# The soft-plus chain and the inner norm roots on GpSimd, an earlier weight split, and another order in the opening

## What is computed

```python
for l in range(DEPTH):                       # first block, DEPTH = 2
    n = rms_norm(h, norm1_w[l])
    proj = einsum('bld,de->ble', n, w_in[l])
    z, xbc, dt_f, dt_b, sc_b, sc_c, sc_v = split(proj)
    y_ssd = ssd_branch(z, xbc, dt_f, dt_b, ...)   # short conv, dt = softplus(dt + bias),
                                                  # a = -exp(a_log) * dt, decays, norm per group
    y_sc = short_conv_branch(sc_b, sc_c, sc_v, ...)
    h = h + einsum('ble,ed->bld', concat(y_ssd, y_sc), w_out[l])
    n = rms_norm(h, norm2_w[l])
    h = h + conv_ffn(n, ...)
...
for l in range(DEPTH):                       # second block
    # conv branch (31 taps, layer_norm), differential attention (rms_norm of each head),
    # block attention, gates, layer_norm, feed-forward with squared relu, layer_norm
```

## Time and profile before

| | |
|---|---|
| median of 3 runs (lowest to highest) | 1765.27 us (1764.46 to 1765.59) |
| the profiled execution's own time | 1764.93 us |
| its span, first to last instruction | 1762.9 us |
| TensorE busy | 1709.6 us (97%), x12334 |
| DVE busy | 1340.2 us (76%) |
| ACT busy | 921.5 us (52%) |
| GpSimd busy | 30.8 us (2%) |
| DMA, mean | 171 GB/s |

### The profile page before, as it was taken

How to read it: one execution, slowest core, us unless ns; L and a number is a source line. 1 busy time by engine, 2 the same in 40 slices (tenths; PEclk the granted TensorE clock), 3 DMA queues, 4 the chain that set the end, 5 groups by cost and what they waited for, 6 DMA issues and landing times.

```text
span 1762.9 us, 30277 instructions
## 1 busy us (share of the span) xinstructions
PE 1709.6 (97%) x12334; PEld 1580.0 (90%) x12342; DVE 1340.2 (76%) x2227; ACT 921.5 (52%) x1481; POOL 30.8 (2%) x51
## 2 busy tenths in 40 slices
PE   7999999999999999999999999999999999999997
PEld 6999889998999979999898998899989989989996
DVE  5867777777877867777798878866678988886666
ACT  5566555555656646555544654444344466453442
POOL 0000000000000000000000001000000000100000
PEclk9999999999999999999999999999999999999999
DMA  6544445555545445555465444555546635455552
GB/s 209 165 144 144 167 146 189 191 185 162 168 145 156 140 164 188 194 186 192 150 215 186 134 154 162 184 191 191 188 147 201 204 122 172 130 197 185 190 191 96
DMA packets 234055, 300.92 MB, mean 171 GB/s; under 512 B 6179, under 2 KB 199357, under 8 KB 233917
## 3 DMA queue, kind: packets, MB, share of 16 engines
q1 hardware_dynamic: 233609, 298.87, 52.0%
q10 hardware_dynamic: 308, 0.12, 0.0%
HBM read 293.72 MB, written 1.05 MB: 167 GB/s over the span
## 4 chain that ended last, share of the span: by engine, by line
PE 76%; DVE 17%; ACT 4%; issue 2%; DMA 0%; ACTq 0%; POOL 0%; DVEq 0%; POOLq 0%
PE bank L489 16%; PE bank L491 16%; PE bank L490 16%; DVE weights_lo L1420 7%; PE bank L567 5%; PE bank L568 5%; PE bank L569 5%; PE bank L539 2%; PE bank L540 2%; PE bank L541 2%; DVE conv_sums L1842 2%; ACT weights_hi L1017 1%; PE bank L689 1%; ACT pair L1280 1%; PE bank L594 1%
## 5 line engine op out<-in xcount | busy, mean ns | idle before, releaser
L489 PE MATMUL bank<-input_hi,weights_hi 128*128 128x256 f32 x2768 | 790.9, 286 | 12.8 <-DVE weights_lo L1420 6.5
L490 PE MATMUL bank<-input_lo,weights_hi 128*128 128x256 f32 x2768 | 783.7, 283 | 0.0
L491 PE MATMUL bank<-input_hi,weights_lo 128*128 128x256 f32 x2768 | 783.5, 283 | 0.0
L1420 DVE TENSOR_TENSOR weights_lo<-raw_weights,weights_hi 128x1024 fp32r<-128x1024 f32 (+1 forms) x554 | 649.8, 1214 | 138.3 <-ACT weights_hi L1017 136.1
L1017 ACT ACTIVATE weights_hi<-raw_weights 128x1024 fp32r<-128x1024 f32 (+1 forms) x554 | 546.3, 1036 | 331.8 <-PE bank L491 175.0
L489 PEld LDWEIGHTS bank<-input_hi,weights_hi 128*128 128x128 f32 x2768 | 531.1, 192 | 21.5 <-issue 17.7
L490 PEld LDWEIGHTS bank<-input_lo,weights_hi 128*128 128x128 f32 x2768 | 531.5, 192 | 1.8
L491 PEld LDWEIGHTS bank<-input_hi,weights_lo 128*128 128x128 f32 x2768 | 531.3, 192 | 0.0
L567 PE MATMUL bank<-weights_hi,hidden_hi 128*128 128x512 f32 x432 | 168.9, 391 | 0.2
L568 PE MATMUL bank<-weights_lo,hidden_hi 128*128 128x512 f32 x432 | 168.7, 390 | 0.0
L569 PE MATMUL bank<-weights_hi,hidden_lo 128*128 128x512 f32 x432 | 168.1, 389 | 0.0
(11 more groups left out here) (256 smaller groups left out, 1795.9 us busy)
## 6 DMA issues: line engine op xcount, KB each, us to landing
raw_weights<-in_w_in SPq DMA_DIRECT2D x105, 1024.0 KB, 5.3
raw_weights<-in_w_ff SPq DMA_DIRECT2D x64, 1024.0 KB, 5.3
raw_weights<-in_w_ffn_up SPq DMA_DIRECT2D x44, 1024.0 KB, 5.1
raw_weights<-in_w_ffn_down SPq DMA_DIRECT2D x22, 1024.0 KB, 5.0
raw_weights<-in_w_out SPq DMA_DIRECT2D x16, 1024.0 KB, 5.1
raw_weights<-in_w_o SPq DMA_DIRECT2D x8, 1024.0 KB, 5.1
pair<-pair SPq DMA_DIRECT2D x64, 64.0 KB, 2.9
raw_weights<-in_w_diff_out SPq DMA_DIRECT2D x4, 1024.0 KB, 5.1
```

The source lines that it names most:

```text
L489: mm(o, w_hi, x_hi, start=first, stop=False, skip_group_check=quiet)
L490: mm(o, w_hi, x_lo, start=False, stop=False, skip_group_check=quiet)
L491: return mm(o, w_lo, x_hi, start=False, stop=last, skip_group_check=quiet)
L1420: tt(wlo[:, t, r], raw[:, s, r], whi[:, t, r].bitcast(f32), SUB).then_inc(w_ready, 1)
```

## The change

The soft-plus steps move from DVE to a function `soft_plus` on GpSimd, ten instructions, with a power of -1 in place of the reciprocal. The thirteen small instructions of an inner norm become one on DVE, a wait, and a power of -0.5 on GpSimd (`spread_roots`). `split_hi(3)` and `split_lo(3)` move from the dt chunk to chunk 0: on ACT behind the middle tap and ahead of the tanh, on DVE behind the outer taps. In the opening TensorE multiplies zeros 20 times, turns the norm's output with ten multiplications of zeros in place of two, and turns the parameter rows after that. On GpSimd the token norms' roots and the clearing of `prow2` take their places between the new functions. Context lines are cut.

```diff
@@ -233,7 +233,8 @@
         small = sb("small", [P, 64])
-        minus_half = small[:, 63:64]
+        minus_half, minus_one = small[:, 56:64], small[0:32, 55:56]
+        spread_var, spread_root = ctx.enter_context(nc.semaphore("spread_var")), ctx.enter_context(nc.semaphore("spread_root"))
         one_hot = sb("one_hot", [P, 32], f32r)
@@ -593,7 +594,7 @@
-            def turned(r):
+            def turned(r, fillers=2):
@@ -603,7 +604,7 @@
                         turn(0, k)
-                keep_clock(2, ring[3])
+                keep_clock(fillers, ring[3])
                 for b in range(4):
@@ -611,18 +612,18 @@
             pe.wait_ge(zero_ready, 2)
-            keep_clock(16, ring[3])
+            keep_clock(20, ring[3])
             pe.wait_ge(ident_loaded, 16)
-            pe.wait_ge(rows_loaded, 16 * N_ROW_DMAS)
-            for l in range(DEPTH):
-                last = nc.tensor.transpose(ring[0][:, l * P:(l + 1) * P], prow[:, 3 * l, :], ident)
-            last.then_inc(pt_ready, 1)
-            keep_clock(4, ring[3])
...
                 cx, ux = l * C1, l * U1
-                turned(l * 2)
+                turned(l * 2, 10 if l == 0 else 2)
+                if l == 0:
+                    pe.wait_ge(rows_loaded, 16 * N_ROW_DMAS)
+                    for i in range(DEPTH):
+                        last = nc.tensor.transpose(ring[0][:, i * P:(i + 1) * P], prow[:, 3 * i, :], ident)
+                    last.then_inc(pt_ready, 1)
                 gemm_paced(0, cx, 0, ux, ring[0], l * 16)
@@ -945,14 +946,43 @@
             pool.memset(minus_half, -0.5).then_inc(half_ready, 1)
+            pool.memset(minus_one, -1.0).then_inc(half_ready, 1)
             pool.memset(in_cols[:], 0.0).then_inc(zero_ready, 1)
...
                     pool.wait_ge(var_ready, r * 2 + t + 1)
-                    nc.gpsimd.tensor_tensor(norm_small[:, 3, t:t + 1], norm_small[:, 2, t:t + 1], minus_half, ALU.pow).then_inc(root_ready, 1)
-            pool.wait_ge(half_ready, 1)
+                    nc.gpsimd.tensor_tensor(norm_small[:, 3, t:t + 1], norm_small[:, 2, t:t + 1], minus_half[:, 0:1], ALU.pow).then_inc(root_ready, 1)
+            def spread_roots(k, n):
+                pool.wait_ge(spread_var, k + 1)
+                nc.gpsimd.tensor_tensor(small[:, 24:24 + n], small[:, 16:16 + n], minus_half[:, 0:n], ALU.pow).then_inc(spread_root, 1)
+            def soft_plus(l):
+                x, u, w, ln, one, den, a = [dts[:, i, :] for i in range(5)] + [dta[:, i, :] for i in range(2)]
+                pool.wait_ge(dt_dve, l * 2 + 2)
+                chain(nc.gpsimd.tensor_scalar(one, w, 1.0, None, ALU.is_equal))
+                chain(nc.gpsimd.tensor_scalar(den, w, -1.0, None, ALU.add))
+                chain(nc.gpsimd.tensor_scalar(x, x, 0.0, None, ALU.max))
+                chain.sync()
+                chain(nc.gpsimd.tensor_tensor(den, den, one, ALU.add))
+                chain.sync()
+                chain(nc.gpsimd.tensor_tensor(den, den, minus_one.to_broadcast([32, SEQ]), ALU.pow))
+                pool.wait_ge(dt_act, l * 2 + 2)
+                chain(nc.gpsimd.tensor_tensor(one, one, ln, ALU.add))
+                chain.sync()
+                chain(nc.gpsimd.tensor_tensor(den, den, u, ALU.mult))
+                chain.sync()
+                chain(nc.gpsimd.tensor_tensor(den, den, one, ALU.mult))
+                chain.sync()
+                chain(nc.gpsimd.tensor_tensor(den, den, x, ALU.add))
+                chain.sync()
+                nc.gpsimd.tensor_scalar(a, den, pc1[0:32, P1["a_exp"]:P1["a_exp"] + 1], -1.0, ALU.mult, ALU.mult).then_inc(dta_ready, 1)
+            chain = Chain(pool, pool_chain)
+            pool.wait_ge(half_ready, 2)
             roots(0)
@@ -963,12 +993,17 @@
-            chain = Chain(pool, pool_chain)
             pool.wait_ge(skip_ready, 2)
-            for r in range(1, 2 * DEPTH - 1):
-                roots(r)
-            pool.wait_ge(y_done, HEADS // 2 * DEPTH)
-            pool.memset(prow2[:], 0.0).then_inc(rows2_zero, 1)
+            for k in range(4 * DEPTH):
+                if k and k % 4 == 0:
+                    roots(k // 2 - 1)
+                    roots(k // 2)
+                if k == 4 * DEPTH - 1:
+                    pool.wait_ge(y_done, HEADS // 2 * DEPTH)
+                    pool.memset(prow2[:], 0.0).then_inc(rows2_zero, 1)
+                if k % 4 == 0:
+                    soft_plus(k // 4)
+                spread_roots(k, TOK)
             pool.memset(hpad[:, :, 0:TAPS - 1], 0.0).then_inc(zero_ready, 1)
@@ -989,6 +1024,8 @@
             for l in range(DEPTH):
+                spread_roots(4 * DEPTH + 2 * l, 8)
+                spread_roots(4 * DEPTH + 2 * l + 1, TOK)
                 for m in range(4):
@@ -1145,7 +1182,6 @@
                         A(dts[:, 1, :], dts[:, 1, :], ACT.Exp).then_inc(dt_act, 1)
-                        split_hi(c + 2, cx, cr)
                         act.wait_ge(dt_dve, l * 2 + 2)
@@ -1156,8 +1192,8 @@
                     last.then_inc(conv_mid, 1)
-                    if 0 < c < 8:
-                        split_hi(c + 2, cx, cr)
+                    if c < 8:
+                        split_hi(c + 2 if c else 3, cx, cr)
                     act.wait_ge(ring_free, ux + (q + RING + 1))
@@ -1432,23 +1468,11 @@
-            def rsqrt_diagonals(sums, n, scale, signal):
-                v, y, t = small[:, 16:16 + n], small[:, 24:24 + n], small[:, 32:32 + n]
-                chain(ts(v, sums, scale, EPS, MUL, ADD))
-                chain.sync()
-                chain(ts(y.bitcast(i32), v.bitcast(i32), 1, None, ALU.arith_shift_right))
-                chain.sync()
-                chain(ts(y.bitcast(i32), y.bitcast(i32), -1.0, MAGIC, MUL, ADD))
-                chain(ts(v, v, -0.5, None, MUL))
-                chain.sync()
-                for _ in range(3):
-                    chain(tt(t, y, y, MUL))
-                    chain.sync()
-                    chain(tt(t, t, v, MUL))
-                    chain.sync()
-                    chain(stt(out=y, in0=t, scalar=1.5, in1=y, op0=ADD, op1=MUL))
-                    chain.sync()
+            def rsqrt_diagonals(k, sums, n, scale, signal):
+                y = small[:, 24:24 + n]
+                ts(small[:, 16:16 + n], sums, scale, EPS, MUL, ADD).then_inc(spread_var, 1)
+                dve.wait_ge(spread_root, k + 1)
                 for i in range(n):
@@ -1577,33 +1601,7 @@
-                x, w, u_, ln = dts[:, 0, :], dts[:, 2, :], dts[:, 1, :], dts[:, 3, :]
-                def steps_of_dt():
-                    one, den = dts[:, 4, :], dta[:, 0, :]
-                    dve.wait_ge(dt_dve, l * 2 + 2)
-                    chain(ts(one, w, 1.0, None, ALU.is_equal))
-                    yield
-                    chain.sync()
-                    chain(stt(out=den, in0=w, scalar=-1.0, in1=one, op0=ADD, op1=ADD))
-                    yield
-                    chain.sync()
-                    chain(V.reciprocal(den, den))
-                    dve.wait_ge(dt_act, l * 2 + 2)
-                    chain(tt(one, one, ln, ADD))
-                    yield
-                    chain.sync()
-                    chain(tt(den, den, one, MUL))
-                    yield
-                    chain.sync()
-                    chain(tt(den, den, u_, MUL))
-                    yield
-                    chain.sync()
-                    chain(stt(out=den, in0=x, scalar=0.0, in1=den, op0=ALU.max, op1=ADD))
-                    yield
-                    chain.sync()
-                    ts(dta[:, 1, :], den, pc1[0:32, P1["a_exp"]:P1["a_exp"] + 1], -1.0, MUL, MUL).then_inc(dta_ready, 1)
+                x, w, u_ = dts[:, 0, :], dts[:, 2, :], dts[:, 1, :]
@@ -1631,7 +1629,7 @@
                     dve.wait_ge(gstat, l * 4 + g + 1)
-                    rsqrt_diagonals(acc[2 + g % 2][:, 0:TOK], TOK, 1.0 / 256, gdiag)
+                    rsqrt_diagonals(l * 4 + g, acc[2 + g % 2][:, 0:TOK], TOK, 1.0 / 256, gdiag)
@@ -1679,17 +1677,14 @@
-                dt_steps = steps_of_dt()
                 for c in range(9):
...
                         stt(out=u_, in0=x, scalar=-1.0, in1=x, op0=MUL, op1=ALU.min).then_inc(dt_dve, 1)
-                        split_lo(c + 2, cx, halves=(0,))
                         dve.wait_ge(dt_act, l * 2 + 1)
                         ts(w, u_, 1.0, None, ADD).then_inc(dt_dve, 1)
-                        split_lo(c + 2, cx, halves=(1,))
                         continue
@@ -1697,14 +1692,8 @@
                                lambda tap, m: p1("xbc_w", 16 * tap + 2 * q + m), ring_free)
-                    if c > DT_CHUNK:
-                        next(dt_steps, None)
-                        next(dt_steps, None)
-                    if 0 < c < 8:
-                        split_lo(c + 2, cx)
-                    if c > DT_CHUNK:
-                        next(dt_steps, None)
-                        next(dt_steps, None)
+                    if c < 8:
```

(5 more changed lines are left out.)

## The result

The changed kernel takes 1819.88 us (median of 4 runs, 1819.72 to 1822.89) against 1765.36 us before: a ratio of 1.0313, 95% interval 1.030 to 1.0326. It is 3.1% slower, where I forecast 1755.7 and gave rival 1, a dear power, 0.22. The profiled execution took 1820.04 us with a span of 1818.2, so 55.3 us were added to the span.

What follows compares the result with a forecast made beforehand. TensorE bounds the kernel, busy 1709.6 of 1762.9 us. Gains 2.45 + 2.7 + 2.65 + 2.7 = 10.5, less 0.6 contention and 0.3 clock, give 9.6 us: 1755.7 us, range 1752 to 1775 (forecast's own 1752.5 to 1759.5).

Steps and rivals of the forecast that it cites:

- rival 1: Soft-plus on GpSimd: power dear, result late, costing twice what exceeds 10.3 us; 1775 at a 20 us power; chance 0.22.
- The power: GpSimd's 32x256 power in soft-plus: about 5 us, between bounds of 1.1 and 90 us, hidden behind chunks 3 to 5.
- the 10.3 us of time in hand: Soft-plus on GpSimd: time left for the power before TensorE needs the result at the end of chunk 5.
- The rival's break-even of 15 us: Soft-plus power on GpSimd: from about 15 us on, the change turns to a loss.
- The opening: Kernel start: twenty multiplications of zeros end at 7.9 to 8.0, `input_lo` starts at 14.1 instead of 16.59; gain 2.45 us.
- The sign that I had named: Opening: the prediction is wrong if the fillers, the ten multiplications between the tokens, run at 0.43 us.
- The split and the soft-plus: Chunks 3 to 5: wait for chunk 3 goes, 1.0 us ahead of chunk 4; gain 2.7 us layer 1, 2.65 layer 0.
- the recurrence: Step-by-step timing of chunks 3 to 5: chunk 5 starts at 464.65 instead of 467.33, in layer 0 46.2 instead of 48.86.
- The norms: Inner norms' roots on GpSimd: TensorE's waits on the diagonals, 1.6 us at L705 and 1.1 at L798, go; gain 2.7 us.
- Contention: DVE's splits beside GpSimd's plain soft-plus work: between 0 and 3.6 us a layer lost, taken as 0.3 a layer.
- The worse reading of it: DVE's splits beside the power: the power would shut them out for its whole length, speaking for the second rival, chance 0.12.

Runs made afterwards that it cites:

- the probe: Kernel before with six extra GpSimd instructions (five powers, one product, of several sizes) where GpSimd idles in layer 0: 1765.01 us.
- the split alone: Kernel before with only the early split of chunk 3: 1764.71 us against 1765.22, ratio 0.9998.
- the roots alone: Kernel before with only the inner norms' roots moved to GpSimd: 1761.74 us, ratio 0.9980.
- the power out: Changed kernel with the 32x256 power turned into a product, leaving out the soft-plus reciprocal: 1755.4 us against 1765.09, ratio 0.9943.
- the reciprocal in the gap: Changed kernel, full version, with comparison, denominator and reciprocal on DVE where it waited for ACT, other six soft-plus instructions on GpSimd: 1755.02 us, ratio 0.9942.
- 96 columns: Changed kernel with the power over the first 96 of 256 columns, the other reciprocals left out: 1773.42 us against 1765.05, ratio 1.0044.
- the soft-plus back on DVE: Changed kernel with the soft-plus steps back in their old places on DVE, other parts kept: 1760.05 us, ratio 0.9972.
- the opening alone: Kernel before with only the new opening: 1763.92 us, ratio 0.9996.

## Why the prediction was wrong

**The power: the step that failed.** "I take about 5 us: above the plain price several times over, nearer to the low end." It took 41.16. The bounds, 1.1 and 90 us, held it; the choice between them did not. The only row had one column, and its excess of 0.35 us over a plain instruction could be set-up or price. The added columns show that 0.159 us of it is paid by each. I let the range end at 1775, as if a power over 20 us need not be covered, though nothing in the trace excluded it. In the sum's terms: the 10.3 us of time in hand were nearly right (9.9 measured, 41.16 - 31.31), and the power's term of 5 us, taken as hidden, was eight times too small.

**The mechanism of rival 1 was right.** It said twice what exceeds 10.3 us, on top of 1755.7. With 41.16 us that is 61.7, so 1817.4, against 1819.9 measured. Missing are the 3.6 us of half clock behind the two stalls, which I had not priced. The rival's break-even of 15 us was too late as well: at 15.66 us the loss is already 8 us, for contention takes 2.1 us a layer of the time in hand and the lower clock another 1.5.

**The opening.** Right in kind, half in size: 1.3 us of 2.45 at `input_lo`. I took the point where the multiplications of zeros pass from 0.43 to about 0.24 us each from one execution. It wanders: sixteen took 5.05 us in that one, and 5.50, 6.20 and 5.29 in three others with the same opening (the probe, the split alone, the roots alone), and twenty took 6.75 to 7.24 us in six. So they end near 9.0 and hold up the first tokens. `input_lo` started between 16.12 and 17.67 with the old opening and between 14.78 and 15.27 with the new one, so the 1.3 us of the two profiled executions are one draw of a gain of 0.9 to 2.9. The sign that I had named, multiplications at 0.43 us, did come, but among the first twenty and not among the ten between the tokens. Alone the opening cannot be told from no change.

**The split and the soft-plus.** Right, step by step: the wait for chunk 3 gone, 0.96 and 0.95 us ahead of chunk 4 where I had 1.0, none ahead of chunk 5. Chunk 5 ends at 50.51 in layer 0; with 5.9 us a chunk it started at 44.6, 4.3 us earlier than before, of which the opening is 1.3 and this part 2.9 (forecast 2.65). In layer 1 it is 2.9 as well (forecast 2.7). That the early split alone is worth next to nothing (0.4 us in layer 1), and that nearly all of the gain needs both, lay in the recurrence but was not said.

**The norms.** 2.7 forecast, 3.5 measured alone, with an interval of 1.9 to 5.1. The powers of 0.70 and 1.65 us were within the bounds. Most of it comes from the first block (1.2 us a layer, where the waits that I added up were 0.8), little from the second (0.25, where they were 0.5); why, stays open.

**Contention.** Both engines slow down: 3.38 against 2.35 us on DVE, 1.58 against 0.71 on GpSimd. The Trainium skill (SBUF — State Buffer, "Who interferes with whom") states that a DVE instruction with two SBUF inputs contends with a GpSimd one that reads SBUF; the trace agrees. The worse reading of it, that the power would shut the splits out, is wrong here: they took 2.35 us beside it.

**The rest of the sum, and some luck.** 1755.7 were forecast for a power that is hidden, 1755.4 measured with the power out and 1755.0 in full with DVE's reciprocal. The terms do not all fit that well: the opening gave about 1.1 us less than its term, the split and the norms about as much more together, and these misses cancel.

## What to carry to other kernels

A function that one instruction evaluates element by element has a price per column that a one-column row cannot show; measure it at the width it will have, in the idle time of its engine, before its result goes on TensorE's path. Where the bounds of such a price lie nearly two powers of ten apart, the time in hand decides, and the chance of missing it belongs near one half. And free a list before moving work up in it: the earlier split gained next to nothing until the soft-plus had left DVE's list.

## What the runs showed that I had not expected

GpSimd's one-operand comparison, sum and maximum with an immediate (L966 to L968) take 0.85 us on 32x256, more than a two-operand sum (0.73), while L982 with a column and an immediate takes 0.47. Partitions do not matter to the power: 32x64 and 128x64 both take 10.5 us. And the same idle time of 2.54 us ahead of the first chunk was followed by a full clock in four profiled executions (the changed kernel, the power out, the reciprocal in the gap, 96 columns) and by the lower clock in two (the soft-plus back on DVE, the opening alone); what decides it stays open. The two are those in which the twenty multiplications of zeros took least, 6.75 and 6.83 us against 6.98 to 7.24, so that the idle time began and ended earliest. In layer 0 the kernel before shows the same: behind 1.8 us of waiting for chunk 3 the clock fell in the executions of the kernel before, the probe and the roots alone, and stayed full in that of the opening alone.
